# Delta rule on one Trainium2 core: the decay scaling of the sample states moved from the inverse to the input projection

## What is computed

```
g = -exp(a_log) * softplus(a_pre + dt_bias)
...
def step(s, inp):
    q_i, qk_i, u_i, w_i, k_i, gl = inp
    v_new = u_i - einsum('bhck,bhkv->bhcv', w_i, s)
    o = einsum('bhck,bhkv->bhcv', q_i, s) + einsum('bhij,bhjv->bhiv', qk_i, v_new)
    s = s * gl[..., None, None] + einsum('bhck,bhcv->bhkv', k_i, v_new)
```

## Time and profile before

| | |
|---|---|
| median of 3 runs | 1590.81 us (1590.49 to 1592.78) |
| profiled execution | 1594.32 us, span 1592.6 us |
| TensorE, matmuls | busy 1563.1 us, 98% of the span |
| VectorE | 1055.5 us, 66% |
| ScalarE | 884.4 us, 56% |
| GpSimd | 256.2 us, 16% |
| granted clock of TensorE over the span | 0.994 of full speed |

### The profile page before, as it was taken

One profiled execution on the slowest core, in us unless ns is written; L12 is line 12 of the kernel. 1 busy time (PEld: TensorE's weight loads), 2 busy tenths in 40 slices (PEclk: granted clock), 3 DMA queues, 4 the chain that ended last, 5 costly groups with the idle time before them and its releaser, 6 DMA issues.

```text
span 1592.6 us, 37769 instructions
## 1 busy us (share of the span) xinstructions
PE 1563.1 (98%) x16212; PEld 1481.5 (93%) x16212; DVE 1055.5 (66%) x1732; ACT 884.4 (56%) x1696; POOL 256.2 (16%) x328
## 2 busy tenths in 40 slices
PE   9999999999999999999999999999999999999997
PEld 7998799999997999999788888999999997999997
DVE  7965686755757877547793747776469837767643
ACT  6856656633645666434652546665358547566433
POOL 7105450000110200003003421100010035400000
PEclk9999999999999999999999999999999999999999
DMA  8941456565753665653635003665569512565550
GB/s 244 292 140 29 134 164 179 183 206 175 255 160 133 200 176 185 195 185 94 189 96 144 20 7 98 176 185 186 186 182 261 174 55 82 165 181 184 188 167 28
DMA packets 245529, 250.10 MB, mean 157 GB/s; under 512 B 16270, under 2 KB 239284, under 8 KB 245300
## 3 DMA queue, kind: packets, MB, share of 16 engines
q1 hardware_dynamic: 237204, 224.78, 46.3%
q0 software_dynamic: 8016, 22.86, 4.9%
q10 hardware_dynamic: 144, 0.05, 0.0%
HBM read 229.75 MB, written 18.32 MB: 156 GB/s over the span
## 4 chain that ended last, share of the span: by engine, by line
PE 92%; ACT 4%; DVE 3%; issue 1%; DMA 0%; SPq 0%; DVEq 0%
PE ps L844 88%; PE ps L848 4%; ACT vk L2053 1%; ACT tri L2053 1%; ACT acts L2053 1%; ACT st L2053 0%; DVE acts L2760 0%; ACT hn L2053 0%; DVE tri L2752 0%; DVE acts L2752 0%; DMA acts<-in_x_sample_dram 0%; ACT L2056 0%; PE ps L1796 0%; DVE st L2760 0%; DVE hn L2760 0%
## 5 line engine op out<-in xcount | busy, mean ns | idle before, releaser
L2752 DVE TENSOR_TENSOR w_mlp<-ring,w_mlp 128x1024 fp32r<-128x1024 f32 x256 | 311.7, 1224 | 119.9 <-ACT w_mlp L2053 113.9
L2053 ACT ACTIVATE w_mlp<-ring 128x1024 fp32r<-128x1024 f32 x256 | 269.4, 1054 | 208.2 <-PE ps L844 208.2
L844 PE MATMUL ps<-hn_split,w_mlp 128*128 128x264 f32 x3072 | 373.3, 284 | 0.0
L844 PE MATMUL ps<-h_split,w_mlp 128*128 128x264 f32 x3072 | 372.6, 283 | 0.0
L844 PEld LDWEIGHTS ps<-hn_split,w_mlp 128*128 128x128 f32 x3072 | 372.0, 188 | 0.3
L844 PEld LDWEIGHTS ps<-h_split,w_mlp 128*128 128x128 f32 x3072 | 371.6, 188 | 0.0
L2053 ACT ACTIVATE tri<-ps 128x264 f32<-128x264 f32 (+4 forms) x222 | 101.4, 463 | 181.2 <-PE ps L844 156.2
L844 PE MATMUL ps<-gdn_hi,w_gdn 128*128 128x264 f32 x896 | 165.8, 285 | 0.0
L844 PEld LDWEIGHTS ps<-gdn_hi,w_gdn 128*128 128x128 f32 x896 | 139.3, 188 | 0.9 <-issue 0.8
L844 PE MATMUL ps<-mixer_lo,w_gdn 128*128 128x264 f32 x448 | 126.9, 283 | 0.0
L2752 DVE TENSOR_TENSOR tri<-tri 128x264 f32<-128x264 f32 (+4 forms) x145 | 59.7, 413 | 101.3 <-ACT h_split L2053 100.6
(11 more groups left out here) (454 smaller groups left out, 2654.2 us busy)
## 6 DMA issues: line engine op xcount, KB each, us to landing
ring<-in_ffn_w_dram SPq DMA_DIRECT2D x128, 1024.0 KB, 5.4
ring<-in_gdn_w_in_dram SPq DMA_DIRECT2D x32, 1024.0 KB, 8.3
ring<-in_ml_w_in_dram SPq DMA_DIRECT2D x12, 1024.0 KB, 5.5
ring<-in_rw_w_rkv_dram SPq DMA_DIRECT2D x12, 1024.0 KB, 5.0
st<-in_state_gdn_S_dram POOLq DMA_DIRECT2D x2, 4096.0 KB, 22.4
ring<-in_gdn_w_out_dram SPq DMA_DIRECT2D x8, 1024.0 KB, 5.0
out_gdn_S_s_dram<-st SPq DMA_DIRECT2D x16, 512.0 KB, 6.8
st<-in_state_mlstm_C_dram POOLq DMA_DIRECT2D x1, 4096.0 KB, 20.5
```

Of the source, the lines that this page charges most:

```text
L844: return nc.tensor.matmul(out, lhsT, rhs, start=start, stop=stop)
L2053: return nc.scalar.activation(out, in_, f, bias=bias, scale=scale)
L2752: return nc.vector.tensor_tensor(out, in0, in1, op)
```

## The change

The samples' decays are computed early: ScalarE takes the exponential of the log decays behind the logarithm in `gate_logs`, GpSimd spreads them on a diagonal, one matmul (hook 6, after tile 13) gives them to all partitions, and VectorE copies them to `E6[:, 5]` after its weight tile of tile 14. GpSimd then scales all eight heads, 8 instructions in a row, before it waits for the norms. Inside the inverse the four scalings of GpSimd and the 32 of ScalarE are gone. Since the state is scaled when key and query read it, two columns of `ccol` are zeroed in the first quadrant, which takes the decay out of `E6[:, 0:2]`, and five matmuls stand where six were.

```diff
                 def sample_products():
                     pe.wait_ge(smp_ok, count.seen(smp_ok))
-                    pe.wait_ge(st_in, count.seen(st_in, 16))
+                    pe.wait_ge(st_sc, count.seen(st_sc, GH))
+                    count.seen(st_in, 16)
...
+                def sample_decays():
+                    pe.wait_ge(egd_ok, count.seen(egd_ok))
+                    b = 6
+                    pe.wait_ge(*last_read[b])
+                    mm(ps[b][:, 0:GH * NS], ones[0:GH, :], rows[0:GH, 1, 0:GH * NS]).then_inc(eg_mm, count.up(eg_mm))
+                    last_read[b] = egs_ev, count.expect(egs_ev)
+                    count.seen(egs_ev)
...
-                    for q in range(6):
-                        last = mm(ps[b][:, P + q * 64:P + (q + 1) * 64], ccol[:, q:q + 1].broadcast_to([P, P]), rtx)
+                    for n, q in enumerate((0, 1, 2, 3, 5)):
+                        last = mm(ps[b][:, P + n * 64:P + (n + 1) * 64], ccol[:, q:q + 1].broadcast_to([P, P]), rtx)
...
                     act(rows[r, 0, 0:T], rows[r, 0, 0:T], ACT.Ln, bias=cst[r, ONE:ONE + 1]).then_inc(gln_ok, count.up(gln_ok))
+                    ac.wait_ge(g_ok, count.seen(g_ok, 4 if j else 1))
+                    act(rows[0:GH, 1, SEQ:T], RG[0:GH, SEQ:T], ACT.Exp).then_inc(eg_ev, count.up(eg_ev))
...
-                def scale_states(h, part):
-                    for s in range(4 * part, 4 * part + 4):
-                        last = act(st[:, s * GH + h, :], st[:, s * GH + h, :], ACT.Copy, scale=E6[:, 4, h * NS + s:h * NS + s + 1])
-                    if part:
-                        last.then_inc(sts_ac, count.up(sts_ac))
...
                 for l in range(1, 5):
-                    fills[l, 0] = lambda l=l: scale_states(3 + l, 0)
                     fills[l, 1] = lambda l=l: value_rows(l - 1)
-                    fills[l, 3] = lambda l=l: scale_states(3 + l, 1)
...
+                    if n == 14:
+                        dv.wait_ge(eg_mm, count.seen(eg_mm))
+                        copy(E6[:, 5], ps[6][:, 0:GH * NS]).then_inc(egs_ev, count.up(egs_ev))
...
                 def add_outer(n):
                     h, _, *banks = OUTER[n]
-                    sc = sts_ac if h > 3 else st_sc
-                    dv.wait_ge(sc, count.seen(sc))
...
                 done(last)
+                done(gp_.memset(ccol[0:32, 0:2], 0.0))
...
+                po.wait_ge(eg_ev, count.seen(eg_ev))
+                gp_.tensor_tensor(hs8(rows[0:GH, 1, 0:GH * NS]), bc(rows[0:GH, 1, SEQ:T], GH, 1), bc(ident[0:GH, 0:GH], NS, 2),
+                                  ALU.mult).then_inc(egd_ok, count.up(egd_ok))
+                po.wait_ge(st_in, count.seen(st_in, 16 * (1 + j)))
+                po.wait_ge(egs_ev, count.seen(egs_ev))
+                for h in range(GH):
+                    s_ = sth[:, h]
+                    gp_.tensor_tensor(s_, s_, bc(E6[:, 5, h * NS:(h + 1) * NS], P, 2), ALU.mult).then_inc(
+                        st_sc, count.up(st_sc))
                 po.wait_ge(rt_ok, count.seen(rt_ok))
...
-                        last.then_inc(qs_ok, count.up(qs_ok))
-                        s_ = sth[:, l - 1]
-                        gp_.tensor_tensor(s_, s_, bc(E6[:, 4, (l - 1) * NS:l * NS], P, 2), ALU.mult).then_inc(
-                            st_sc, count.up(st_sc))
+                        last.then_inc(qd_ok, count.up(qd_ok))
```

More of the change, by code:

```diff
@@ L432, in hybrid_trunk @@
         smp_ok = semaphore("smp_ok")
-        sts_ac = semaphore("sts_ac")
+        eg_ev = semaphore("eg_ev")
         taps_ok = semaphore("taps_ok")
@@ L449, in hybrid_trunk @@
         ssq_ok = qs_ok
+        egd_ok = qs_ok
+        qd_ok = st_sc
+        eg_mm = kk_mm
+        egs_ev = s_ok
         sums_mm = ct_mm
@@ L1179, in gdn @@
                 split_linear(gdn_hi, mixer_lo, 4 * D, evacuated, hnl_ok, banks=4, raw=gdn_raw[j], paired={(6, 5)[j]: lambda: norm(hn, KT - 2)},
-                             hooks={0: conv_states, 2.5: gates, 5: log_decays_to_columns, 7: cumulate_decays, 11: sum_squares, 13: decay_exponents,
+                             hooks={0: conv_states, 2.5: gates, 5: log_decays_to_columns, 6: sample_decays, 7: cumulate_decays, 11: sum_squares, 13: decay_exponents,
                                     14: query_exponents, 15: grams})
@@ L1352, in gdn @@
                     if c == 1:
-                        pe.wait_ge(qs_ok, count.seen(qs_ok, 4))
+                        pe.wait_ge(qd_ok, count.seen(qd_ok, 4))
                     query_state(c)
@@ L2316, in gdn @@
                         act(gl[:], ps[7][:, 64:96], ACT.Exp)
-                        act(E6.rearrange("p q n -> p (q n)"), ps[7][:, P:512], ACT.Exp).then_inc(cols_ok, count.up(cols_ok))
+                        act(E6[:, 0:5].rearrange("p q n -> p (q n)"), ps[7][:, P:P + 5 * 64], ACT.Exp).then_inc(cols_ok, count.up(cols_ok))
                     if n in (29, 30):
@@ L2354, in gdn @@
                 for l in range(1, 5):
-                    fills[l, 0] = lambda l=l: scale_states(3 + l, 0)
                     fills[l, 1] = lambda l=l: value_rows(l - 1)
-                    fills[l, 3] = lambda l=l: scale_states(3 + l, 1)
                 fills[1, 1] = lambda: (sample_squares(), value_rows(0))
-                fills[1, 3] = lambda: (sample_norm(), scale_states(4, 1))
+                fills[1, 3] = sample_norm
                 invert64(fills, X6, Z6)
@@ L2389, in gdn @@
                 solved_values(1)
-                ac.wait_ge(st_sc, count.seen(st_sc, 4))
+                ac.wait_ge(qd_ok, count.seen(qd_ok, GH + 4))
                 weight_hi()
@@ L3040, in gdn @@
                         nc.vector.tensor_reduce(rep[:, GH + n:GH + n + 1], odd, AX.XY, ALU.add)
-                tt(khp.rearrange("p g (h a n) -> p (g h) a n", h=4, a=4), bc(ks_, 4, 2), bc(hs8(E6[:, 5]), 4, 2), ALU.mult)
+                tt(khp.rearrange("p g (h a n) -> p (g h) a n", h=4, a=4), bc(ks_, 4, 2), bc(hs8(E6[:, 4]), 4, 2), ALU.mult)
                 step(tt(vv[:, :, 0:NS], vs_, hs8(E6[:, 3]), ALU.mult))
```

## The result

The changed kernel is slower, and by more than predicted: 1613.46 us, the median of 5 runs (1611.30 to 1619.65), against 1590.49 us for the kernel before, run beside it (5 runs, 1589.84 to 1592.78). The ratio is 1.0144, with a 95% interval of 1.0122 to 1.0167: +23 us, where +8.2 was forecast and 1604.0 us was the upper end of the range. The profiled execution took 1611.30 us with a span of 1609.6, so 17.0 us more span than the profiled one before.

What follows compares the result with a forecast made beforehand. TensorE was taken as the bound, running 92% of the span's chain. Terms: 5.7 (tile 11 stalls) + 0 (inverse) + 0 (matmuls) + 0.8 (turns) + 1.7 (clock) = +8.2 us on 1590.81, giving 1599.0 us; range 1593.0 to 1604.0.

Steps and rivals of the forecast that it cites:

- The stall at tile 11: Projection, layers 0 and 3: ScalarE's wait for g_ok delays TensorE by 3.3 and 2.4 us, together +5.7 us.
- The inverse: Removing ScalarE's and GpSimd's scalings there gives back 0, between zero and 3.6 us, as TensorE does not wait for them.
- the row of level 5: Inverse: with ScalarE idle, the copy of X starts 0.77 us after its products, against 0.76 in level 4.
- The extra matmul, memsets and copies: Projection: one matmul more, one less in the exponents, small GpSimd and VectorE work hidden: 0, between -0.2 and +0.4 us.
- The turns between GpSimd and VectorE: Projection: GpSimd's eight products take turns with VectorE's two-input operations: +0.8 us, range 0 to 3.4.
- the worst case: VectorE's loss to GpSimd's products per layer: 8 x 0.3 + 2.8 = 5.2 us, up to 1.7 us of stall.
- with every turn lost, 3.4 us: Projection: by the exclusive-lock rule alone, the turns term is 3.4 us, not 0.8, and the whole sum below 10.8.
- The clock: TensorE's clock falls to half once behind the two tile 11 stalls: +1.7 us, between 0 and 3.4.
- Rival 2: No fall of TensorE's clock behind the stalls: sum 6.5 us, 1597.3 us; chance 0.2.
- Rival 1: Projection: both stalls followed by a clock fall and VectorE loses every turn: +12.5 us, 1603.3 us; chance 0.2.
- Rivals 3 and 4: 3: tile 11 wait covered, 1591 us, chance 0.12; 4: inverse tied to ScalarE, -3.6, 1587.2 us, chance 0.06.
- The lower end of the range: Whole kernel: 1593.0 us, given for stalls half as long and no clock fall.

Runs made afterwards that it cites:

- logs_early: Changed kernel with VectorE's pair of log decays behind the taps of tile 5 instead of tile 6: 1608.03 us, ratio 1.0102.
- before_no_scalings: Kernel before with the inverse's scalings on ScalarE and GpSimd cut to one of 128 columns, nothing put in the projection: 1590.78 us, ratio 1.0002.
- all_three: Changed kernel with log decays behind tile 5's taps, the small exponential behind tile 7's copies and weight tile, GpSimd's products in quarters: 1592.38 us, ratio 1.0002.
- half_pieces: Changed kernel with each of GpSimd's eight products cut in two, 16 instructions of four samples: 1600.75 us, ratio 1.0066.
- quarter_pieces: Changed kernel with each of GpSimd's eight products cut into four pieces of two samples, 32 instructions: 1600.80 us, ratio 1.0058.
- one_input: The kernel turns_alone with GpSimd's eight products replaced by multiplications of the same state by the constant 1.0, one tensor read: 1591.77 us, ratio 1.0004.
- no_scalings: Changed kernel with each of GpSimd's eight products in the projection cut to one of 128 columns, all waits kept: 1601.46 us, ratio 1.0061.
- turns_alone: Changed kernel with log decays behind tile 5's taps and the small exponential behind tile 7's copies and weight tile, products whole: 1603.87 us, ratio 1.0086.
- exp_later: Changed kernel with ScalarE's wait for g_ok and the 8x8 exponential put behind tile 7's copies and weight tile: 1603.73 us, ratio 1.0079.

## Why the prediction was wrong

**The stall at tile 11: right.** Forecast 3.3 + 2.4 us; measured 3.10 + 2.90. ScalarE's wait was 3.76 us in layer 0 (3.73 forecast) and released by VectorE, and the queue carried it on as described. logs_early showed that one follows the other, in layer 0: 2.55 us less wait, 2.58 us less stall.

**The inverse: right.** Forecast 0; before_no_scalings gave 0.0002 +- 0.0009 of the time. The argument was the row of level 5, where the copy is as late without scalings as with them.

**The extra matmul, memsets and copies: right** as far as it can be told: all_three has every one of them and costs nothing that shows.

**The turns between GpSimd and VectorE: this step failed.** The forecast was +0.8 us with a range of 0 to 3.4; the measured idle time is 8.2 us. The place was right, the first stall before tile 21, and the slack was right: 0.65 + 2.8 = 3.45 us a layer by the prediction, and 7.3 us of excess less 4.1 of stall leaves 3.2. What VectorE loses was wrong. I set 0.3 us for a subtraction, from a picture in which VectorE asks for its turn 1.43 us into a product and waits for the rest; the phases are not tied, and three subtractions in layer 0 lost 0.28, 1.04 and 1.41 us. I left out the copy of the convolution's columns, which reads one SBUF tile and lost 1.69 us. The two other products lost 1.59 and 1.25, which the worst case had right at 1.4 each. By parts the worst case of 5.2 us was thus 2.4 for the subtractions (measured 2.7), 2.8 for the two products (2.8) and nothing for the copy (1.7): it came in full, with the copy on top. So two choices failed. The copy was missing from the list, 1.7 us a layer. And of the 1.7 us of stall a layer that the worst case left I took 0.4, because both products would have to lose their turn; no row said how likely that was, and in every trace with whole products at this place both did.

Of the page cited there (the Trainium skill, SBUF — State Buffer, section "SBUF: two separate sides") the exclusive turn, held for an instruction, is what half_pieces and quarter_pieces show for GpSimd's product of two tensors. For the one-tensor form the measurement differs: the page has a VectorE operation with two SBUF inputs wait for any GpSimd operation that reads SBUF and began first, and in one_input GpSimd read the states and eight subtractions passed at 1.21 to 1.23 us. The page counts in VectorE's operations in a 2-port mode too, beside those with two SBUF inputs; that would fit the copy, which I had passed over, though no run shows which mode it ran in. What I made of it, "with every turn lost, 3.4 us", was my own sum with the copy missing.

**The clock: right in kind, short in size.** One fall of 1.7 us was forecast. The profiled execution lost 2.8 us more than the one before; by the mean clocks of the medians it is about 8. Of the 14.8 us by which the forecast was short, the turns are 7.4, the clock some 6.4 by that estimate and tile 11 is 0.3. Behind the stalls of 2.9 to 3.4 us at tile 11 the clock fell each time, eight times in four traces (the changed kernel, no_scalings, half_pieces, quarter_pieces; granted clock 0.50 to 0.66 over the 3 to 7 us behind them). The stalls of 2.6 us before tile 22 sometimes drew a fall and sometimes not. In the changed kernel's execution no fall followed the 2.59 us at 98.35, but one did in turns_alone, behind the same stall, as the window shows:

```profile
91.00:96.00 5.00, 3.49 (x18) 3.49 (x19) 4.86 (x9) 2.21 (x5) 0.00 (x0) 0.66 0.23 64
```

With six stalls of 1.5 us and more in place of the two that I counted, each another chance, the median pays for several. That part follows from the failed step, but not all: no_scalings has only the two stalls that I counted, and it was 4.2 us above its idle time where I had 1.7. Why the clock falls behind one stall of 2.6 us and not behind another stays open. Rival 2 (no fall) is refuted by the windows behind tile 11.

**The rivals.** Rival 1 had the right direction (both stalls with a fall, every turn lost) and the wrong prices: +12.5 against +23. Rivals 3 and 4 did not occur. The lower end of the range, 1593.0 us, is 0.7 below what it is said to be (1590.81 + 5.7 / 2 = 1593.7). The condition named as what would make the prediction wrong, a stall from tile 20 on that is longer than those at tile 11, is what happened in sum: 4.1 us a layer before tiles 21 and 22, though no single one was longer.

## What to carry to other kernels

Before work is put on GpSimd beside a VectorE that has little slack, list every VectorE instruction in the stretch that multiplies or subtracts two SBUF tiles, and the copies from SBUF to SBUF (here the reduction and the taps with an operand in PSUM lost nothing), charge each with up to the length of one GpSimd instruction, and compare the sum with the slack; the sum of the busy times does not show this cost. If the place must stay, cut GpSimd's instructions into pieces: here halves already removed 7 of the 8 us of idle time, and two halves took GpSimd 2.09 us in place of 1.90. And a wait put into an in-order queue costs whatever stands behind it; give the value earlier or take it later in the queue, and do both if one tile's work doesn't cover it.

## What was not expected of the hardware

- A copy with one SBUF source and an SBUF target waits like an operation on two tensors: 0.32 us became 2.01.
- GpSimd's product with the constant 1.0 took 2.78 us for 128x1024 floats (tensor_scalar, one tensor read; median of eight) and the one of two tensors 1.90, yet the slower one let VectorE's subtractions pass.
- Idle times of TensorE of 2.6 us were followed by a fall of its clock in some executions and not in others, at the same place of the program (granted clock 1.00 over 92 to 99 us in the changed kernel, 0.66 over 5 us in turns_alone and exp_later).
